# Half of an output projection multiplied inside a softmax branch

## What is computed

```python
# 8 heads of retention, 8 heads of sparse attention, 64 wide each
ret = retention(rq, rk, rv, positions) * silu(rg)        # 512 wide
o = g_cmp * o_cmp + g_slc * o_slc + g_win * o_win         # three softmax branches
att = o * silu(ng)                                        # 512 wide
mixed = concatenate([ret, att])                           # 1024 wide
y = rmsnorm(mixed @ w_out, g_post)                        # "projection 2"
x = x + gate * y
# second block begins
f = (silu(u @ w_gate) * (u @ w_up)) @ w_down              # u = rmsnorm(x, g_ffn1_pre)
```

## Time and profile before

| what | value |
| --- | --- |
| median of 3 runs | 1502.58 us (1501.13 to 1503.46) |
| span of the profiled execution, first to last instruction | 1500.5 us |
| what lies around the span (median less span) | 2.1 us |
| mean granted clock of TensorE | 0.992 of 2.4 GHz |
| PE, DVE, ACT, POOL busy | 97, 55, 46, 13% of the span |
| softmax branch (scores 0 to the last value matmul) | 253.76 to 355.51 us |
| projection 2 and the first four MLP chunks | 355.51 to 428.17 us |

### The profile page before, as it was taken

How to read it: one execution, slowest core, us unless ns; L and a number is a source line. 1 busy time by engine, 2 the same in 40 slices (tenths; PEclk the granted TensorE clock), 3 DMA queues, 4 the chain that set the end, 5 groups by cost and what they waited for, 6 DMA issues and landing times.

```text
span 1500.5 us, 22048 instructions
## 1 busy us (share of the span) xinstructions
PE 1452.3 (97%) x8524; PEld 1226.9 (82%) x8524; DVE 828.7 (55%) x1455; ACT 683.7 (46%) x1302; POOL 201.9 (13%) x319
## 2 busy tenths in 40 slices
PE   7999999899999999999999999989999999999997
PEld 4887876678988888888998777769988888888996
DVE  6678646776645444432275577574754444422474
ACT  4565536676542222221363556676532232321563
POOL 0000000443310000000130222451300000000221
PEclk9999999999999999999999999999999999999999
DMA  9542440004033333333404211503133333332321
GB/s 365 197 167 85 124 157 10 1 2 169 2 99 98 98 98 98 94 95 94 152 3 167 71 57 43 169 16 99 33 109 98 94 92 96 103 105 92 120 85 56
DMA packets 42148, 146.71 MB, mean 98 GB/s; under 512 B 4673, under 2 KB 7121, under 8 KB 41682
## 3 DMA queue, kind: packets, MB, share of 16 engines
q1 hardware_dynamic: 37986, 128.99, 27.2%
q0 software_dynamic: 3072, 15.71, 2.8%
q10 hardware_dynamic: 1008, 0.89, 0.2%
HBM read 141.39 MB, written 4.19 MB: 97 GB/s over the span
## 4 chain that ended last, share of the span: by engine, by line
PE 84%; DVE 9%; ACT 3%; issue 2%; DMA 1%; POOL 0%; DVEq 0%; SPq 0%; ACTq 0%; POOLq 0%
PE B L285 22%; PE B L287 22%; PE B L286 22%; PE CROW_P L285 3%; PE CROW_P L287 3%; PE CROW_P L286 3%; PE B L1789 2%; PE B L2025 1%; DVE AL L1381 1%; DVE WADA L1143 1%; PE CROW_P L1868 1%; ACT T L622 1%; PE CROW_P L1768 1%; ACT AH L622 1%; DVE WL L1110 1%
## 5 line engine op out<-in xcount | busy, mean ns | idle before, releaser
L285 PE MATMUL B<-UH,WH 128*128 128x512 f32 (+1 forms) x1008 | 374.7, 372 | 4.6 <-DVE WL L1110 3.7
L287 PE MATMUL B<-UH,WL 128*128 128x512 f32 (+1 forms) x1008 | 372.3, 369 | 0.0
L286 PE MATMUL B<-UL,WH 128*128 128x512 f32 (+1 forms) x1008 | 372.3, 369 | 0.0
L622 ACT ACTIVATE WH<-RAW 128x1024 fp32r<-128x1024 f32 x174 | 182.6, 1052 | 120.0 <-DMA RAW<-in_stream 111.6
L285 PEld LDWEIGHTS B<-UH,WH 128*128 128x128 f32 x1008 | 190.4, 189 | 38.0 <-issue 5.0
L286 PEld LDWEIGHTS B<-UL,WH 128*128 128x128 f32 x1008 | 190.3, 189 | 32.0
L287 PEld LDWEIGHTS B<-UH,WL 128*128 128x128 f32 x1008 | 190.2, 189 | 32.0
L1110 DVE TENSOR_TENSOR WL<-RAW,WH 128x1024 fp32r<-128x1024 f32 x94 | 116.0, 1240 | 143.8 <-ACT WH L622 143.7
L1462 DVE TENSOR_TENSOR WL<-RAW,WH 128x1024 fp32r<-128x1024 f32 x80 | 98.0, 1226 | 76.7 <-ACT WH L622 73.9
L622 ACT ACTIVATE T<-B 128x256 f32<-128x256 f32 (+5 forms) x186 | 86.5, 465 | 109.9 <-PE B L287 63.3
L622 ACT ACTIVATE T<-T 128x512 f32<-128x512 f32 (+3 forms) x131 | 68.7, 525 | 130.8 <-DVE T L1466 119.2
(11 more groups left out here) (419 smaller groups left out, 3146.2 us busy)
## 6 DMA issues: line engine op xcount, KB each, us to landing
RAW<-in_stream SPq DMA_DIRECT2D x202, 512.0 KB, 3.7
WADA<-in_w_ada SPq DMA_DIRECT2D x8, 1024.0 KB, 16.7
RAW<-in_stream SPq DMA_DIRECT2D x16, 384.0 KB, 3.5
WADA<-in_w_ada SPq DMA_DIRECT2D x2, 2048.0 KB, 11.5
W<-in_w POOLq DMA_DIRECT2D x2, 2048.0 KB, 12.1
X<-in_x SPq DMA_DIRECT2D x2, 1024.0 KB, 11.0
DECAY<-in_decay POOLq DMA_DIRECT2D x1, 2048.0 KB, 9.6
X<-in_x POOLq DMA_DIRECT2D x2, 1024.0 KB, 8.2
```

The lines of the kernel that those rows point to most:

```text
L285: nc.tensor.matmul(out, lh, rh, start=start, stop=False, **kw)
L286: nc.tensor.matmul(out, lh, rl, start=False, stop=False, **kw)
L287: return nc.tensor.matmul(out, ll, rh, start=False, stop=stop, **kw)
L622: return nc.scalar.activation(out, in_, func, **kw)
```

## The change

Retention's half of projection 2 (tiles 0 to 3) is multiplied in the rounds of the softmax branch, 512 columns at a time: `part_step(c, k)` does contraction tile k of output chunk c into bank B5, one step in each of the rounds 5 to 9 and 12 to 35, between transposes and values; three steps are left for behind the last round. After four steps ACT copies B5 to PART[c] (`part_out`). The softmax branch keeps three score banks, and its scores wait for the exponential of the first unit of the round before. The weights of projection 2 are loaded by half: four chunks with the columns of retention's half (two output chunks each), then four with attention's; ACT and DVE split them from round 4 on. `mix_out` multiplies attention's half in halves of tokens, tiles 4 and 6 of six chunks first, then 5 and 7; DVE adds PART and evicts (`whole`), ACT squares the result. The MLP's first four chunks run with the contraction tile in the outer loop (`first_up`), with the sum for the second half's norm behind the last tile. The second block's softmax keeps its four banks.

```diff
-        KEPT_AT = {"p1": (64, 72, 80, 88), "p2": (16, 24, 64, 72, 80, 32, 40, 88), "p6": ("w0", "w1", 64, 72, 0, 32, 40, 8),
+        KEPT_AT = {"p1": (64, 72, 80, 88), "p2": ("w0", 16, 24, "w0", 16, 24, 64, 72), "p6": ("w0", "w1", 64, 72, 0, 32, 40, 8),
...
+        PART = [at(f"PART{m}", OFF_U + ((16 if m < 4 else 0) + 2 * (m % 4)) * KB, [P, SEQ]) for m in range(8)]
...
-        S_BANK, PT_BANK = [B[2], B[3], B[4], B[5]], [B[6], B[7]]
+        S_BANK, PT_BANK = {"nsa": [B[2], B[3], B[4]], "band": [B[2], B[3], B[4], B[5]]}, [B[6], B[7]]
...
+        PART_ROUNDS = [5, 6, 7, 8, 9] + list(range(12, 36))
+        PART_STEPS = [(c, k) for c in range(8) for k in range(4)]
+        PART_AT = {m: PART_STEPS[n] for n, m in enumerate(PART_ROUNDS)}
+        PART_LEFT = PART_STEPS[len(PART_ROUNDS):]
+        PART_ENDS = {m: c for m, (c, k) in PART_AT.items() if k == 3}
+        def out_weights(m, k):
+            hi, lo = KEPT[KEPT_AT["p2"][m // 2 + (4 if k >= 4 else 0)]]
+            cols = slice((4 * (m % 2) + k % 4) * P, (4 * (m % 2) + k % 4 + 1) * P)
+            return hi[:, cols], lo[:, cols]
...
+                if D_P2 <= d < D_P2 + 8:
+                    half, pair = divmod(d - D_P2, 4)
+                    sp.dma_start(RAW[:, slot, :].rearrange("p (m c) -> p m c", m=2),
+                                 a["stream"][D_P2 + 2 * pair:D_P2 + 2 * pair + 2, :, 512 * half:512 * half + 512].rearrange("m p c -> p m c")
+                                 ).then_inc(raw_here[slot], 16)
+                    return
...
-            sums(0, SHORT)
+            sums(0, [("y", 1), ("y", 2), ("y", 3), ("n", 1), ("y", 4), ("n", 2), ("y", 5), ("n", 3), ("y", 6), ("n", 4), ("n", 5), ("n", 6)])
...
+            def part_out(c):
+                wait(act, E["part"], c + 1)
+                E["part_out"].mark(f(PART[c][:, :], B[5][:, :], ACT.Copy))
...
+                            if tag is NSA and s == 0 and m in PART_ENDS:
+                                part_out(PART_ENDS[m])
+                    elif tag is NSA and m in PART_ENDS:
+                        part_out(PART_ENDS[m])
...
+                if m == 4:
+                    hi_of_weights(D_P2)
+                if m == 9:
+                    hi_of_weights(D_P2 + 1)
+                if m == 14:
+                    wait(act, E["gn_lo"], 4)
+                    hi_of_weights(D_P2 + 2)
+                if m in (19, 27, 34):
+                    hi_of_weights(D_P2 + 3 + (m - 19) // 7)
...
+                if m == 35:
+                    hi_of_weights(D_P2 + 6)
                 if m == 37:
-                    hi_of_weights(D_P2 + 4)
-                    hi_of_weights(D_P2 + 5)
-                if m in (29, 31):
-                    hi_of_weights(D_P2 + (m - 29) // 2)
-                if m == 35:
-                    hi_of_weights(D_P2 + 2)
-                    hi_of_weights(D_P2 + 3)
-
-            softmax_pairs(NSA_UNITS, NSA, nsa_ahead)
+                    for c in range(len(PART_ENDS), 8):
+                        part_out(c)
+                    hi_of_weights(D_P2 + 7)
...
+            def mix_out():
+                table_set(EXP_LN_SET)
+                for m in range(8):
+                    wait(act, E["y_copy"], m + 1)
+                    y_square(0, m, Y_H[:, m, cols_of(0)])
+                    if 2 <= m < 6:
+                        hi_of_weights(D_F1 + m - 2)
+                y_rms(0)
+                for m in range(8):
+                    wait(act, E["y_copy"], 8 + m + 1)
+                    y_square(1, m, Y_H[:, m, cols_of(1)])
+                    for k in ((), (), (), (0,), (1,), (2,), (3,), (4,))[m]:
+                        next_hi(0, k, VECS[:, V_F1PRE:V_F1PRE + 8])
+                for k in range(5, KT):
+                    next_hi(0, k, VECS[:, V_F1PRE:V_F1PRE + 8])
+                y_rms(1)
...
+                if m == 5:
+                    gn_m(3)
+                    lo_of_weights(D_P2)
                 if m == 6:
                     gn_lo(2)
-                    gn_m(3)
-                if m == 9:
+                if m == 7:
                     gn_lo(3)
+                if m in (10, 15, 20, 28, 35):
+                    lo_of_weights(D_P2 + (10, 15, 20, 28, 35).index(m) + 1)
+                if m == 37:
+                    lo_of_weights(D_P2 + 6)
+                    lo_of_weights(D_P2 + 7)
...
+            def mix_out(gain, scale):
+                def whole(t, m):
+                    h = cols_of(t)
+                    if t == 0:
+                        wait(dve, E["half"], m + 1)
+                    else:
+                        dve.wait_ge(mm, D_P2 + m + 1)
+                    E["y_copy"].mark(tt(Y_H[:, m, h], B[uses["p2", 8 * t + m][0]][:, h], PART[m][:, h], ALU.add))
+                wait(dve, E["part_out"], 8)
+                for m in range(8):
+                    whole(0, m)
+                    if 3 <= m < 7:
+                        lo_of_weights(D_F1 + m - 3)
+                whole(1, 0)
+                whole(1, 1)
+                dve.wait_ge(x_again, 32)
+                wait(dve, E["y_rstd"], 1)
+                for n in range(KT + 2):
+                    if n < 6:
+                        whole(1, n + 2)
+                    next_u(0, n, Y_H, gain, scale)
+                wait(dve, E["y_rstd"], 2)
+                for n in range(KT + 2):
+                    next_u(1, n, Y_H, gain, scale)
+                wait(dve, E["n_rstd"], 2)
...
+            def part_step(c, k):
+                if k == 0:
+                    pe.wait_ge(w_lo, D_P2 + c // 2 + 1)
+                    wait(pe, E["part_out"], c)
+                if c == 0:
+                    wait(pe, E["gn_lo"], k + 1)
+                hi, lo = out_weights(c, k)
+                ins = mm3(B[5][:, :], hi, lo, MRH[:, k, :], MRL[:, k, :], k == 0, k == 3)
+                if k == 3:
+                    E["part"].mark(ins)
...
-                        outs = [S_BANK[(2 * m + s) % 4] for s in range(2)]
-                        wait(pe, tag["max" if pair[0]["bias"] is not None else "exp"], 2 * m - 2)
+                        outs = [banks[(2 * m + s) % len(banks)] for s in range(2)]
+                        if tag is NSA:
+                            wait(pe, tag["exp"], 2 * m - 1)
+                        else:
+                            wait(pe, tag["max"], 2 * m - 2)
...
+                    if tag is NSA and m in PART_AT:
+                        part_step(*PART_AT[m])
...
+            for c, k in PART_LEFT:
+                part_step(c, k)
+            def mix_chunk(m, t, tiles, done):
+                h = cols_of(t)
+                for k in tiles:
+                    if t == 0 and m == 0:
+                        wait(pe, at_lo, {4: 1, 6: 2, 5: 3, 7: 4}[k])
+                    hi, lo = out_weights(m, k)
+                    ins = mm3(B[uses["p2", 8 * t + m][0]][:, h], hi, lo, UH[:, k, h], UL[:, k, h], k == 4, k == 7)
+                if done is mm:
+                    ins.then_inc(mm, 1)
+                elif done is not None:
+                    done.mark(ins)
+            def mix_out():
+                for m in range(6):
+                    wait(pe, *((NSA["exp"], 64), (NSA["exp"], 62), (at_x, 7), (at_x, 8), (NSA["lo"], 64), (E["part_out"], 8))[m])
+                    pe.wait_ge(w_lo, D_P2 + 4 + m // 2 + 1)
+                    mix_chunk(m, 0, (4, 6), None)
+                for m in range(6):
+                    mix_chunk(m, 0, (5, 7), E["half"])
+                for m in range(6, 8):
+                    bank_of("p2", m)
+                    pe.wait_ge(w_lo, D_P2 + 4 + m // 2 + 1)
+                    mix_chunk(m, 0, (4, 6, 5, 7), E["half"])
+                for m in range(8):
+                    bank_of("p2", 8 + m)
+                    mix_chunk(m, 1, (4, 6, 5, 7), mm)
+                    if m == 1:
+                        y_stats(0)
...
+            def first_up(phase, d0, t, done):
+                h = cols_of(t)
+                for k in range(KT):
+                    wait(pe, E["nu_lo"], 8 * t + k + 1)
+                    for j in range(4):
+                        if k == 0 and done is None:
+                            bank_of(phase, j)
+                            pe.wait_ge(w_lo, d0 + j + 1)
+                        ins = mm3(B[j][:, h], wtile(WH, d0 + j, k), wtile(WL, d0 + j, k), UH[:, k, h], UL[:, k, h], k == 0, k == KT - 1)
+                        if k == KT - 1 and done is mm:
+                            ins.then_inc(mm, 1)
+                    if k == 3 and done is None:
+                        y_stats(t + 1)
+                    if k == 3 and done is mm:
+                        n_stats(t - 1)
+                if done is mm:
+                    n_stats(t)
+            def mlp_up(phase, d0, n0, t, by_tile=False):
+                if by_tile:
+                    first_up(phase, d0, t, None)
+                    first_up(phase, d0, t + 1, mm)
...
-            wait(pe, E["gn_lo"], 4)
```

(40 more changed lines are left out.)

34 lines of the change are left out of this document (12 added, 22 removed).

## The result

The changed kernel takes 1511.9 us (median of 4 runs, 1510.87 to 1513.68) where the kernel before takes 1501.87 beside it: ratio 1.0067, interval 1.0053 to 1.0081, 10 us slower. The forecast was slower, 1509.5, with a range to 1515.5. Direction and most terms hold; the size is 3 us short (+6.9 forecast, +10.0 measured).

A forecast was written before the change was run, and what follows sets the result against it. TensorE, busy for 97% of the span, was taken as the bound. Rounds 0 to 11 (+5.3), rounds 12 to 35 (+14.1) and the part behind the branch (-12.5) sum to +6.9 us: median 1509.5 us, range 1499 to 1515.5.

The forecast's parts named there:

- Rounds 12 to 35: Softmax branch: 24 steps of 0.71 us less 3.9 of covered waits, plus 1.0 for three banks: +14.1 us.
- The six rounds with a bank wait: Rounds 12, 14, 20, 22, 28, 30: scores wait 0.15 us each for an exponential, 2.87 us from scores to scores.
- Rounds 0 to 11: Start of the softmax branch, bound by DVE: bank wait, late maxima and the first step waiting for its weight low, +5.3 us.
- Behind the branch: Last value matmul to the MLP loop: matmuls moved away, four new waits and a stall, loop begins 12.5 us sooner.
- UL of tile 3: DVE behind projection 2's second half: adds ahead of next_u, beside POOL's sums, make PE wait for this, +1.3 us.
- the small waits of 0.6 and 0.3: Second half of the MLP start: first UL after the reciprocal root, +0.6 us; POOL's six last sums, +0.3.
- the sum over the first half: Projection 2: weight highs and lows between the adds, POOL's sums beside them, make PE wait here, +1.9 us.
- The stall before the loop: Last sum now just before the MLP loop: its root, table load, high and low no longer hidden, 4.7 us stall.
- the MLP loop, taken at no cost: The steady MLP loop behind the stall: forecast difference 0.
- A: Rival: waits behind the branch are covered, first rounds cost only their five steps; +1.0 us, 1503.6; chance 0.24.
- B: Rival: steps fill TensorE's idle time and open none, rounds grow 11.5 us; -5.1 us, 1497.5; chance 0.14.
- C: Rival: the bank wait binds in every round, 0.3 us each, +6 us; 1515.5; chance 0.11.

The follow-up runs named there:

- Experiment 3: The kernel before with only the three score banks and their wait in the first softmax branch, no steps: 1508.39 us, ratio 1.0039 to the kernel before.
- Experiment 4: The changed kernel with its first weight chunk split earlier, in rounds 0 and 1 instead of 4 and 5: 1508.66 us, ratio 1.0040 to the kernel before.
- experiment 8: The changed kernel with DVE's four MLP weight lows behind all eight adds of the first half: 1513.47 us, ratio 1.0074 to the kernel before.
- experiment 9: The changed kernel with DVE's MLP weight lows one behind add 5, one behind add 6, two behind add 7: 1513.24 us, ratio 1.0069 to the kernel before.
- experiment 2: The kernel before with only the last sum over features moved from behind chunk 1 to behind chunk 3: 1509.9 us, ratio 1.0051.
- experiment 6: The changed kernel with the last sum behind tile 4 instead of 7 and POOL's last sums not waiting for the last UL: 1513.51 us, ratio 1.0070.
- experiment 1: The changed kernel with 18 unread 512-column matmuls filling PE's stall before the MLP loop: 1510.44 us, ratio 1.0052 to the kernel before.
- experiment 10: The changed kernel with four score banks kept for rounds 0 to 4, three from round 5: 1516.85 us, ratio 1.0089 to the kernel before.

## Why the prediction was right, and where it fell short

**Rounds 12 to 35 (+14.1, came 14.0).** The steps start 0.78 us ahead of what follows them and hide 0.08 of start gaps: 0.70, where I took 0.71 (rounds 16, 18, 24 and 26 take 2.78 us from scores to scores instead of 2.08). The waits for AL vanished. The six rounds with a bank wait take 2.91 us (forecast 2.87), a wait of 0.20 each instead of 0.15: 2.91 less 2.01 and 0.70. Experiment 3 shows what the sum hid: without steps the bank costs 4.7 here, and the steps fill most of it: these six rounds take 2.91 there as well, so a step in them costs nothing on top of the bank.

**Rounds 0 to 11 (+5.3, came +6.4).** Counted from scores 0, the replay holds up to the first step: scores 1 late by 1.23 (1.15), maximum 5 (at 271.68) by 2.96 (2.95), and the step runs at 271.82, which is 273.04 on the old kernel's count (273.0). What comes behind does not: scores 6 are 6.2 late (4.7). The clock was at its lower level: the step itself took 1.08 us to the next start instead of 0.78, and the 24 value matmuls behind it start 0.107 apart instead of 0.06, 1.1 us. Experiment 4 takes the wait away, the clock stays at 1.00 and 3.2 of the 6.4 us go; it does not part the wait from the clock.

**Behind the branch (-12.5, came -12.7).** Two of my reasons were wrong at about the right size, and that the total agrees to 0.2 is partly luck: counted by starts the waits ahead of the stall were 3.2 us instead of 4.1, and the rest came 0.7 longer than I had it. The wait of 1.4 us at the start of the MLP is not for UL of tile 3 but for DVE's adds, which free the banks; and the small waits of 0.6 and 0.3 did not come. The wait of 1.5 us for the sum over the first half (1.9) is there, but it is not worth 1.5: experiment 8 took it away, a new one of 0.5 came at the start of the MLP, and about 0.6 us were left of it by the trace. POOL's sums set it, in turns with DVE (experiment 9). The adds, which I charged nothing beside POOL, indeed kept 0.42 us (the one at 387.18, inside POOL's sum of 386.39 to 387.86). The stall before the loop is 4.63 (4.7), and the reason I gave can make it alone (experiment 2), but it was half the reason here: the load behind the slots was nearly as late (experiment 6).

**The step that failed: the MLP loop, taken at no cost.** "Now 0.9 of it is its own matmuls and 4.7 is a stall": I priced a stall by its length. The clock fell to 0.50 with it, and the first twelve loop matmuls took 0.427 us each: +2.4, shown by experiment 1, where the stall is filled and the loss gone. The size of this term varies: the eight traces with such a stall have a loop of 218.95 to 220.36 us (+1.6 to +3.0), the five with no wait in front of it 217.40. With the 1.1 us of rounds 0 to 11 it is the 3 us by which I was short: 6.9 + 2.4 + 1.1 = 10.4 against 10.0.

**The rivals.** A (waits covered) is out: they came. B needed under 2 us in rounds 0 to 11 and three banks that bind nowhere; both fail. C (a bank wait in every round) comes nearest in a kernel without steps, with waits in 11 of the rounds (experiment 3), and is not true of this one. That an edit moving 20 us of matmuls can still lose is accounted for so: moved work gains only what idle time it fills, at most 7.8 us here; the bank costs 6, the stall before the loop and its clock 7, the late first weight 3 and the waits in between 3.

## What to carry to other kernels

Price a PE stall of some microseconds twice: its length, and the half clock behind it (here 4.6 us cost 6.2 to 7.6). Before work is moved into another stage, take away there alone the resource that it will need and look at the price. And where an outer loop is turned, list what each inner unit used to release on its way: here the slots for the next loads were held to the end, and the sum of the norm came last as well.

## What the runs showed of the hardware

- Behind a wait of PE of 4.6 us the granted clock was 0.50 in the first 4.86 us of the loop in the changed kernel and in experiment 2, 1.00 in experiment 1 with matmuls in the gap. In experiment 4 it was 0.68 over the same 4.86 us, with the same wait of 4.6: the loss in the loop goes from 1.6 to 3.0 us.
- The 2.60 us before the first step were followed by matmuls at twice their distance. Shorter waits went either way. At the start of the MLP a wait of 1.7 us was followed by a clock of 0.52 for 3.4 us in experiment 8 and by one of 0.52 and 0.57 in 9 and 10, but by 1.00 in experiments 1, 4 and 6; behind 1.4 us in the changed kernel (405.21) it was 1.00. So in these traces the length of such a wait does not by itself tell which clock follows.
- The Trainium skill (TensorE: Matmul & The Clock Gate, Part 1: The HAM clock gate) has TensorE fall to 1.2 GHz when it idles and return only after it has been busy. The traces agree in what they show: 0.50 of 2.4 GHz is that level, and the filler holds it off.
- The same code can meet either clock from one execution to the next: 0.66 from 205 to 215 us in the profile of experiment 10, a like stretch in that of 9, 1.00 in that of the changed kernel. Such a stretch is 4 us, as much as the edits tested here, so an edit that is worth one or two was read from segments of the trace rather than from the median, and those too had to be compared at the same clock.
